# The second scan direction's steps put out eight steps behind the first one's

## The chip, the cores and the metric

The kernel runs on one core of one Trainium2 chip. The metric is the device time of one launch in microseconds (us), the median of the runs. All engines of the core are used: TensorE (PE) multiplies, VectorE (DVE) and ScalarE (ACT) take the products out of the eight PSUM banks, and SyncE (SP) issues the weight transfers. GpSimd does nothing here.

## What is computed

The reference is two transformer blocks of two layers each, over 256 tokens and, in the second block, 256 more of context. The change touches one stage of the second block's first layer, a linear recurrence with a matrix state that is scanned forwards and backwards over the 512 tokens, 8 heads of width 64:

```python
def wkv7_scan(S0, inputs, reverse):
    def step(S, inp):
        r, w, k, v, kk, a = inp
        S = (S * w[:, :, None, :]
             - jnp.einsum('bhvk,bhk->bhv', S, kk)[..., None] * (kk * a)[:, :, None, :]
             + v[..., None] * k[:, :, None, :])
        return S, jnp.einsum('bhvk,bhk->bhv', S, r)
    ...
S_cf, y_cf = wkv7_scan(S0, dir_inputs(f_ctx, 0), reverse=False)
S_cb, y_cb = wkv7_scan(S0, dir_inputs(f_ctx, 1), reverse=True)
_, y_lf = wkv7_scan(S_cf, dir_inputs(f_lat, 0), reverse=False)
_, y_lb = wkv7_scan(S_cb, dir_inputs(f_lat, 1), reverse=True)
o_lat = rwkv7_readout(y_lf + y_lb, f_lat, r_k, gn_w, gn_b)
```

The two directions share nothing until their outputs are added.

## The kernel before

The program is a list of stages (`schedule`), and each engine runs its own part of each stage, in the order in which it is written out; at a stage's end all engines meet at a barrier. Nothing reorders work: what one engine has put in a row, it does in that row, and a wait holds everything behind it on that engine.

The recurrence stage is `wkv`. It cuts the 512 tokens into 4 pairs of chunks of 64 tokens. In each direction, every pair is first **prepared** and then **advanced** through.

Preparing a pair takes 17 steps. `tokens` (L1104) transposes two operands, taken out by ACT. Six `products` steps follow (L1117), called p00, p01, p10, p11, p20, p21 here (the kind, then the half). ACT copies a part of p00 and p01 and DVE masks the rest; after p01 DVE also makes four wide masks (L2078 to L2081), and only then is level 0 ready. Then a 64x64 triangular inverse is built in five levels. Each level is an `inner` step (PE at L1092, then ACT's copy at L1563) and an `outer` step (PE at L1092, then DVE's two subtractions at L2106 and L2108). The outer needs the inner's copy, and the next inner needs DVE's subtractions. DVE also makes a mask in each inner (L2097).

Advancing takes 8 steps: `x` (L1154, L1161), `u` (L1165), `state` (L1170, L1171) and `y` (L1176, L1181, L1183), for each of the two chunks. u needs ACT's copy of x, state needs ACT's copy of u and is taken out by DVE (L2117, L2119), x of the next chunk needs that state.

`one_way` writes the steps of one direction: it prepares pair 0, and then puts the 17 preparing steps of the next pair between the 8 advancing steps of this one. That makes 100 steps a direction, 25 for each of the first three pairs' advance, 17 before them and 8 behind them. With x0, u0, s0, y0 for the first chunk's steps, x1, u1, s1, y1 for the second's, and in1, out1 and so on for the levels, a period of 25 reads

```
x0 tokens p00 | u0 p01 p10 | s0 p11 p20 | y0 p21 in1 | x1 out1 in2 | u1 out2 in3 | s1 out3 in4 | y1 out4 in5 out5
```

`wkv_order` merges the two directions (L686 to L688), and PE, ACT and DVE all three walk through its list. Before the change every step of direction 0 is followed at once by the same step of direction 1. Each step takes the next of the eight PSUM banks in turn, and PE waits before a step until that bank has been read by ACT or DVE. The step that is meant is written with its direction below, as in in2(0).

In the rows of the trace, a buffer's name tells the direction: sq, rs, tmp, rstd, rec_kt, rec_rt, rec_lw and ms belong to direction 0; mix_small, rec_lora, rec_spare, rec_kk, rec_r and rec_k to direction 1.

Of the kernel before, what the change touches and what calls it, by code (L numbers as in the profile page):

```python
# [404 lines left out]
def build(nc, ins, out):  # L405
    order = weight_order()
    with ExitStack() as ctx:
# [253 lines left out]
        def wkv_order():  # L661


            def prepare(i):
                yield ("tokens", i)
                for k in range(3):
                    for half in range(2):
                        yield ("products", i, k, half)
                for lvl in range(1, LEVELS):
                    for what in ("inner", "outer"):  # L670
                        yield (what, i, lvl)

            def advance(i):
                for n in range(2):
                    for what in ("x", "u", "state", "y"):
                        yield (what, i, n)

            def one_way():
                yield from prepare(0)
                for i in range(4):  # L680
                    ahead = list(prepare(i + 1)) if i < 3 else []
                    for k, this in enumerate(advance(i)):
                        yield this
                        yield from ahead[len(ahead) * k // 8:len(ahead) * (k + 1) // 8]

            for step in one_way():  # L686
                for d in range(2):
                    yield (d, *step)  # L688


        def by_head(h):
# [40 lines left out]
        def _(pe):  # L732
# [351 lines left out]
            def wkv():  # L1084

                def small(bank, lhs, rhs, part=lambda t: t):
# [6 lines left out]
                    return mm  # L1093

                for d, what, i, *more in wkv_order():
                    pair, halves, way, vt = wkv_pairs(d)[i], wkv_halves(d), scan[d], ph3["vt"]
                    lw, bt, kt, rt = way["lw"], way["bt"], way["kt"], way["rt"]
# [112 lines left out]
        def _(act):  # L1210
# [329 lines left out]

            def wkv():
                for d, what, i, *more in wkv_order():
                    halves, way = wkv_halves(d), scan[d]
                    if what == "tokens":
# [68 lines left out]
        def _(dve):  # L1613
# [439 lines left out]
            def wkv():  # L2053
# [6 lines left out]

                begun = set()
                for d, what, i, *more in wkv_order():
                    way, st = scan[d], scan[d]["state"]
                    nt, m, mt, b = way["nt"], way["m"], way["mt"][i % 2], way["b"]
# [213 lines left out]
```

## Time and profile before

| | us |
|---|---|
| median of 3 runs | 3096.91 |
| lowest and highest run | 3082.44, 3098.36 |
| the profiled execution | 3097.93 |
| its span on the core | 3096.1 |
| PE busy | 2667.8 (86%) |
| DVE busy | 1522.3 (49%) |
| ACT busy | 897.5 (29%) |
| the recurrence stage on PE, from its first to its last weight load | 1460.1 to 1724.5 |

Times below are counted from the span's start. PEld is the row of TensorE's weight loads: every matmul has one ahead of it, and the loads are issued in program order, so their starts show when PE came to a step. An f32 matmul of 64 rows is two records in the trace. A bracket at a row's end says how long the engine had stood idle and for whom. The granted clock is TensorE's, as a share of 2.4 GHz: 1.00 is 2.4 GHz and 0.50 is 1.2 GHz, and means between them mix the two.

### The profile page before, as it was taken

Reading aid. Unit: us, or ns where it says so; the run is one execution under the profiler, and the core shown is the slowest. Engines: PE = TensorE matmul, PEld = TensorE weight load, DVE = VectorE, ACT = ScalarE, POOL = GpSimd, SP = SyncE. Lnnn points to the kernel's source line nnn. Section 1 sums busy time; section 2 is a strip of 40 time slices with the busy share of each in tenths; the row PEclk is TensorE's granted clock in tenths of the full one; section 3 lists DMA queues with packets and bytes.
Section 4 is the critical chain, followed back from the end, with each engine's and each line's share of the span. In section 5 each row is a group of like instructions: output and inputs, shape, how many; then the busy total and the mean of one; then the engine's idle time right before and its main releaser. Section 6 shows DMA issues by size and latency. Waiting matters only on the chain.

```text
span 3096.1 us, 41660 instructions
## 1 busy us (share of the span) xinstructions
PE 2667.8 (86%) x17514; PEld 2078.2 (67%) x17514; DVE 1522.3 (49%) x2510; ACT 897.5 (29%) x1541; POOL 0.2 (0%) x4
## 2 busy tenths in 40 slices
PE   6947788688999967973999789999899998979898
PEld 5715666366888744742999448887688875736897
DVE  4674554715553255778444455542333323285544
ACT  1132011314222234334222132222422223244543
POOL 0000000000000000000000000000000000000000
PEclk9967989799999987976899899999999999989999
DMA  6700554033433220320000124332222222101443
GB/s 252 270 2 29 202 205 189 14 109 109 150 136 123 95 97 1 123 95 1 3 4 4 55 109 143 131 135 102 75 95 96 94 96 83 68 1 55 150 165 135
DMA packets 43418, 309.72 MB, mean 100 GB/s; under 512 B 4704, under 2 KB 6112, under 8 KB 6368
## 3 DMA queue, kind: packets, MB, share of 16 engines
q1 hardware_dynamic: 41328, 300.24, 26.7%
q10 hardware_dynamic: 1904, 6.80, 0.6%
q8 instruction: 140, 2.29, 0.3%
q14 instruction: 46, 0.38, 0.0%
HBM read 305.98 MB, written 1.05 MB: 99 GB/s over the span
## 4 chain that ended last, share of the span: by engine, by line
PEld 29%; PE 23%; DVE 12%; issue 10%; ACT 6%; DMA 0%; PEldq 0%; DVEq 0%; ACTq 0%
PEld bank L1031 10%; PEld bank L1038 10%; PEld bank L1034 9%; PE bank L1092 3%; PE bank L862 3%; PE bank L938 1%; ACT hn L1370 1%; PE bank L957 1%; PE bank L1031 1%; DVE ms L1644 1%; PE bank L1034 1%; PE bank L1038 1%; ACT w_hi L1346 1%; PE bank L988 1%; PE bank L835 1%
## 5 line engine op out<-in xcount | busy, mean ns | idle before, releaser
L1727 DVE TENSOR_TENSOR w_lo<-ring,w_hi 128x1024 fp32r<-128x1024 f32 (+1 forms) x264 | 315.0, 1193 | 639.1 <-ACT w_hi L1346 639.1
L1031 PE MATMUL bank<-ffn_x_hi,w_hi 128*128 128x512 f32 (+1 forms) x1344 | 498.2, 371 | 4.8 <-DVE w_lo L1727 3.8
L1034 PE MATMUL bank<-ffn_x_lo,w_hi 128*128 128x512 f32 (+1 forms) x1344 | 493.9, 367 | 0.0
L1038 PE MATMUL bank<-ffn_x_hi,w_lo 128*128 128x512 f32 (+1 forms) x1344 | 493.8, 367 | 0.0
L1644 DVE SCALAR_TENSOR_TENSOR ms<-ring,c_silu 128x1024 f32<-128x1024 f32 x288 | 352.1, 1223 | 98.0 <-DMA ring<-in_stream 93.0
L1346 ACT ACTIVATE w_hi<-ring 128x1024 fp32r<-128x1024 f32 (+1 forms) x264 | 271.6, 1029 | 336.6 <-PE bank L1034 323.3
L1031 PEld LDWEIGHTS bank<-ffn_x_hi,w_hi 128*128 128x128 f32 x1344 | 253.1, 188 | 58.0 <-DVE w_lo L1727 10.9
L1034 PEld LDWEIGHTS bank<-ffn_x_lo,w_hi 128*128 128x128 f32 x1344 | 253.1, 188 | 46.3
L1038 PEld LDWEIGHTS bank<-ffn_x_hi,w_lo 128*128 128x128 f32 x1344 | 253.1, 188 | 46.3
L1031 PE MATMUL bank<-ffn_h_hi,w_hi 128*128 128x512 f32 (+1 forms) x704 | 263.2, 374 | 1.5 <-DVE w_lo L1727 1.0
L1038 PE MATMUL bank<-ffn_h_hi,w_lo 128*128 128x512 f32 (+1 forms) x704 | 258.6, 367 | 0.0
L1034 PE MATMUL bank<-ffn_h_lo,w_hi 128*128 128x512 f32 (+1 forms) x704 | 258.6, 367 | 0.0
L862 PE MATMUL bank<-hn,ring 128*128 128x256 f32 (+1 forms) x784 | 184.4, 395 | 20.2 <-DMA ring<-in_stream 8.9
L862 PEld LDWEIGHTS bank<-hn,ring 128*128 128x128 f32 x784 | 151.0, 195 | 53.1 <-issue 16.8
L1031 PEld LDWEIGHTS bank<-ffn_h_hi,w_hi 128*128 128x128 f32 x704 | 132.5, 188 | 29.6 <-DVE w_lo L1727 3.1
L1034 PEld LDWEIGHTS bank<-ffn_h_lo,w_hi 128*128 128x128 f32 x704 | 132.6, 188 | 25.4 <-issue 1.4
L1038 PEld LDWEIGHTS bank<-ffn_h_hi,w_lo 128*128 128x128 f32 x704 | 132.6, 188 | 24.2
L1481 ACT ACTIVATE ffn_h_hi<-rs 128x512 fp32r<-128x512 f32 (+1 forms) x88 | 50.9, 579 | 326.0 <-DVE rs L1967 326.0
L1475 ACT ACTIVATE sq<-bank 128x512 f32<-128x512 f32 (+1 forms) x88 | 47.9, 545 | 246.1 <-PE bank L1038 246.1
L1967 DVE TENSOR_TENSOR rs<-bank,sq 128x512 f32<-128x512 f32 (+1 forms) x88 | 54.9, 624 | 85.1 <-PE bank L1038 55.3
L1816 DVE SCALAR_TENSOR_TENSOR x<-bank,modv,x 128x256 f32<-128x256 f32 x80 | 35.8, 480 | 117.0 <-PE bank L862 70.8
L835 PE MATMUL bank<-mix_in_x_hi,mix_in_w_hi 128*128 128x512 f32 x152 | 63.6, 418 | 25.4 <-DVE mix_in_x_lo L1745 18.6
(413 smaller groups left out, 3743.6 us busy)
## 6 DMA issues: line engine op xcount, KB each, us to landing
ring<-in_stream SPq DMA_DIRECT2D x283, 1024.0 KB, 4.8
x<-in_x SPq DMA_DIRECT2D x1, 2048.0 KB, 8.6
one_const<-in_one ACTq DMA_DIRECT2D x1, 1665.0 KB, 11.1
mix_const<-in_two ACTq DMA_DIRECT2D x1, 1440.0 KB, 6.1
win_const<-in_win ACTq DMA_DIRECT2D x1, 1089.0 KB, 5.0
c_silu<-in_c SPq DMA_DIRECT2D x1, 1024.0 KB, 10.6
out<-hn ACTq DMA_DIRECT2D x1, 1024.0 KB, 4.8
mix_small<-in_small_two ACTq DMA_DIRECT2D x1, 768.0 KB, 7.6
```

Source lines behind the costliest of these rows:

```text
L835: mm = pe.matmul(bank[:, :], high[:, kc, :], hi, start=kc == 0, stop=False)
L862: mm = pe.matmul(bank[:, 0:tok], w[:, kc * COLS + m * P:kc * COLS + (m + 1) * P], a[:, kc, 0:tok], start=kc == 0, stop=kc == KC - 1)
L1031: mm = pe.matmul(bank[:, 0:tok], high[:, kc, :], hi, start=k == 0, stop=False)
L1034: mm = pe.matmul(bank[:, 0:tok], high[:, kc, :], lo, start=False, stop=False)
L1038: mm = pe.matmul(bank[:, 0:tok], low[:, kc, :], hi, start=False, stop=last)
L1092: mm = pe.matmul(part(bank[r, col]), lhs[r, col], part(rhs[r, col]), start=True, stop=True)
L1346: nc.scalar.activation(place(n)[0][:, 0:h.nk, :], raw_half(h), ACT.Copy).then_inc(sem("w_hi_ready"), 1)
L1475: nc.scalar.activation(ffn_gate[:, h.c % 2, 0:tok], bank[:, 0:tok], ACT.Silu).then_inc(sem("gate_ready"), 1)
L1481: nc.scalar.activation(ph5["h_hi"][:, h.c, 0:tok], ffn_hidden[:, h.c % 2, 0:tok], ACT.Copy).then_inc(sem("hidden_hi"), 1)
L1644: link(V.scalar_tensor_tensor(ms2[:].rearrange("p a b -> p (a b)"), w, 1.0, c_silu[:, part % 2, :], ALU.mult, ALU.mult, accum_out=dst))
L1727: V.tensor_tensor(low[:, 0:h.nk, :], raw_half(h), high[:, 0:h.nk, :].bitcast(F32), ALU.subtract).then_inc(sem("w_split"), 1)
L1967: V.tensor_tensor(ffn_hidden[:, h.c % 2, 0:tok], bank[:, 0:tok], ffn_gate[:, h.c % 2, 0:tok], ALU.mult).then_inc(sem("product_ready"), 1)
```

## The change

```diff
-            for step in one_way():
-                for d in range(2):
-                    yield (d, *step)
+            steps = list(one_way())
+            lag = len(list(prepare(0))) // 2
+            for k in range(len(steps) + lag):
+                if k < len(steps):
+                    yield (0, *steps[k])
+                if k >= lag:
+                    yield (1, *steps[k - lag])
```

`prepare(0)` has 17 steps, so the lag is 8. The first 8 steps of direction 0 and the last 8 of direction 1 have no partner; in between, step k of direction 0 is followed by step k - 8 of direction 1. The steps, their instructions and the order within each direction stay as they are. All lines below L692 move down by four.

On PE at the start of the stage, from the last of the products on, there stands before

```order
L1117 MATMUL bank<-rec_r,rec_bt 64x64 x8
L1092 MATMUL bank<-sq,rs 64x64 x16
L1092 MATMUL bank<-mix_small 64x64 x16
L1092 MATMUL bank<-rs,tmp 64x16x2 x16
L1092 MATMUL bank<-tmp,rs 64x16x2 x16
L1092 MATMUL bank<-rec_lora,rec_spare 64x16x2 x16
L1092 MATMUL bank<-rec_spare,rec_lora 64x16x2 x16
L1092 MATMUL bank<-sq,rs 64x64 x16
```

and now

```order
L1121 MATMUL bank<-rec_rt,rec_bt 64x64 x16
L1096 MATMUL bank<-sq,rs 64x64 x16
L1096 MATMUL bank<-rs,tmp 64x16x2 x16
L1096 MATMUL bank<-tmp,rs 64x16x2 x16
L1108 MATMUL bank<-base,rec_k 128x128 x4
L1108 MATMUL bank<-base,rec_bt 128x128 x4
L1096 MATMUL bank<-sq,rs 64x64 x16
L1121 MATMUL bank<-rec_kk,rec_bt 64x64 x8
L1121 MATMUL bank<-rec_bt,rec_kk 64x64 x8
```

Between in1(0) and out1(0) the other direction's in1 is gone and nothing stands in its place; between out1(0) and in2(0) there are the transposes of direction 1 and no longer its out1.

On PE in the period of a later pair, around x1(0) and in2(0), there stands before

```order
L1154 MATMUL bank<-rec_vt,mix_o 64x64 x8
L1161 MATMUL bank<-mix_const,rec_kt 64x64 x8
L1154 MATMUL bank<-rec_vt,rec_spare 64x64 x8
L1161 MATMUL bank<-ring,rec_kk 64x64 x8
L1092 MATMUL bank<-rs,rstd 64x16x2 x16
L1092 MATMUL bank<-rstd,rs 64x16x2 x16
L1092 MATMUL bank<-rec_lora,rec_spare 64x16x2 x16
L1092 MATMUL bank<-rec_spare,rec_lora 64x16x2 x16
L1092 MATMUL bank<-sq,rs 64x64 x16
```

and now

```order
L1158 MATMUL bank<-rec_vt,mix_o 64x64 x8
L1165 MATMUL bank<-mix_const,rec_kt 64x64 x8
L1121 MATMUL bank<-rec_kk,rec_bt 64x64 x8
L1121 MATMUL bank<-rec_bt,rec_kk 64x64 x8
L1096 MATMUL bank<-rs,rstd 64x16x2 x16
L1096 MATMUL bank<-rstd,rs 64x16x2 x16
L1121 MATMUL bank<-rec_kk,rec_k 64x64 x8
L1121 MATMUL bank<-rec_r,rec_k 64x64 x8
L1096 MATMUL bank<-sq,rs 64x64 x16
```

p01(1) has come to stand ahead of out1(0), and p10(1), not out1(1), is what lies between out1(0) and in2(0).

On DVE at the same place, the subtractions of out1(0) (tile rstd) are reached before through

```order
L2097 TENSOR_TENSOR rs<-sq,mix_const 128x512
L2097 TENSOR_TENSOR mix_small<-mix_const 128x512
L2106 TENSOR_TENSOR sq<-sq,bank 128x128x2
L2108 TENSOR_TENSOR rstd<-rstd,bank 128x128x2
L2106 TENSOR_TENSOR mix_small<-mix_small,bank 128x128x2
L2108 TENSOR_TENSOR rec_spare<-rec_spare,bank 128x128x2
```

and now through

```order
L2101 TENSOR_TENSOR rs<-sq,mix_const 128x512
L2079 TENSOR_TENSOR mix_small<-bank,mix_const 128x256
L2082 TENSOR_TENSOR rec_spare<-mix_const 128x512
L2083 SCALAR_TENSOR_TENSOR mix_small<-mix_small,mix_const 128x512
L2084 TENSOR_TENSOR mix_small<-mix_const 128x512
L2085 SCALAR_TENSOR_TENSOR rec_spare<-rec_spare,mix_const 128x512
L2110 TENSOR_TENSOR sq<-sq,bank 128x128x2
L2112 TENSOR_TENSOR rstd<-rstd,bank 128x128x2
```

The five operations of p01(1), its part and the four wide masks, now stand directly ahead of the subtractions of out1(0).

## Rows read from the trace of the kernel before

**Rows 1.** The profile's 40 slices of 77.4 us: PE busy, granted clock, in tenths.

```profile
PE   6947788688999967973999789999899998979898
...
PEclk9967989799999987976899899999999999989999
```

**Rows 2.** Windows over the stage, by pair: us, busy by engine, clock, DMA.

```profile
1460.10:1512.10 52.00, 49.12 (x1297) 47.98 (x1297) 24.46 (x52) 10.48 (x19) 0.00 (x0) 0.83 0.01 3
1512.10:1576.70 64.60, 62.33 (x1745) 60.41 (x1744) 29.09 (x62) 14.62 (x26) 0.00 (x0) 0.95 0.01 4
...
1706.50:1724.60 18.10, 17.71 (x445) 16.75 (x443) 4.67 (x11) 4.14 (x7) 0.00 (x0) 1.00 0.01 3
```

**Rows 3.** Who weight loads waited for in the stage: us in total, times, longest.

```profile
PEld bank L1176 <- DVEq L2089: 4.3, 3, 1.7
PEld bank L1092 <- issue: 3.8, 15, 0.3
...
PEld bank L1092 <- DVEq L2089: 2.5, 1, 2.5
```

**Rows 4.** Timeline of weight loads at pair 1: start us, us, what.

```profile
1541.85 1.02 PEld L1092 LDWEIGHTS bank<-rec_lora,rec_spare 64*64 64x64 f32 x32
...
1543.72 1.02 PEld L1092 LDWEIGHTS bank<-sq,rs 64*64 64x64 f32 x32
1544.99 1.04 PEld L1092 LDWEIGHTS bank<-mix_small 64*64 64x64 f32 x32 [0.25 <-issue]
1545.95 0.89 PEld L1165 LDWEIGHTS bank<-ms,tmp 64*64 64x64 f32 x14
```

**Rows 5.** Timeline of DVE behind out1(1) at 1543.7 us.

```profile
1543.96 0.42 DVE L2106 TENSOR_TENSOR mix_small<-mix_small,bank 128x256 f32<-128x256 f32 x1 [1.11 <-PE bank L1092]
1544.30 0.42 DVE L2108 TENSOR_TENSOR rec_spare<-rec_spare,bank 128x256 f32<-128x256 f32 x1
```

**Rows 6.** Timeline of ACT behind in2(1) at 1545.95 us.

```profile
1546.20 0.60 ACT L1563 ACTIVATE rec_lora<-bank 128x512 f32<-128x512 f32 x1 [0.69 <-PE bank L1092]
```

**Rows 7.** Timeline of weight loads at x0(0), x0(1) and p00.

```profile
1507.84 1.01 PEld L1154 LDWEIGHTS bank<-rec_vt,mix_o 64*64 64x64 f32 x16
...
1509.80 0.19 PEld L1154 LDWEIGHTS bank<-rec_vt,rec_spare 64*64 64x64 f32 x2
...
1513.97 0.54 PEld L1117 LDWEIGHTS bank<-rec_kt,rec_bt 64*64 64x64 f32 x16 [0.17 <-issue]
...
1514.90 0.55 PEld L1117 LDWEIGHTS bank<-rec_kk,rec_bt 64*64 64x64 f32 x16
```

**Rows 8.** Timeline of DVE at p01(0)'s and p01(1)'s parts and behind.

```profile
1519.26 0.42 DVE L2075 TENSOR_TENSOR sq<-bank,mix_const 128x256 f32<-128x256 f32 x1 [2.06 <-ACT sq L1559]
...
1522.68 0.42 DVE L2075 TENSOR_TENSOR mix_small<-bank,mix_const 128x256 f32<-128x256 f32 x1 [0.22 <-DVE rstd L2081]
...
1525.19 0.68 DVE L2081 SCALAR_TENSOR_TENSOR rec_spare<-rec_spare,mix_const 128x512 f32<-128x512 f32 x1
1526.02 0.76 DVE L2086 TENSOR_TENSOR mix_o<-bank,mix_const 128x256 f32<-128x256 f32 x2
```

**Rows 9.** Timeline of weight loads at p20(1), y0(0) and y0(1).

```profile
1525.02 0.55 PEld L1117 LDWEIGHTS bank<-rec_r,rec_bt 64*64 64x64 f32 x16
1526.89 0.55 PEld L1176 LDWEIGHTS bank<-rec_rt,mix_const 64*64 64x64 f32 x16 [1.31 <-DVEq L2089]
...
1528.56 0.86 PEld L1176 LDWEIGHTS bank<-rec_r,ring 64*64 64x64 f32 x15
```

**Rows 10.** Windows between changes of the granted clock, columns as in Rows 2.

```profile
1474.10:1487.70 13.60, 12.92 (x242) 12.93 (x244) 8.00 (x19) 1.79 (x3) 0.00 (x0) 0.50 0.01 2
...
1528.70:1535.50 6.80, 6.72 (x132) 6.54 (x126) 5.03 (x13) 0.34 (x1) 0.00 (x0) 0.50 0.01 2
...
1593.50:1600.40 6.90, 6.83 (x132) 6.64 (x130) 5.13 (x13) 0.60 (x1) 0.00 (x0) 0.51 0.01 2
...
1658.40:1665.20 6.80, 6.73 (x131) 6.54 (x126) 5.00 (x13) 0.39 (x1) 0.00 (x0) 0.50 0.01 2
```

## The prediction

> **What bounds the kernel now.** I read the page's 40 slices first. The stage lies in slices 19 to 22 (1460 to 1725 us), with PE busy in 7 to 9 tenths there and the clock between 0.8 and 0.9 [rows 1]. So PE is the bound of the stage, and time can only come or go by PE's waits and by its clock. The windows by pair say the same: of the 64.6 us of a period PE is busy for 62.3, while DVE has 29.1 and ACT 14.6, and the clock's mean is 0.95 [rows 2]; the period repeats three times, within 0.4 us. Then I read what PE waits for. In the list of waits of the weight loads there are three of up to 1.7 us at y0 for a bank that DVE still holds, fifteen of some 0.25 us before an inner, and one of 2.5 us before the first inner [rows 3]. Last I read the clock: it stood at 1.2 GHz for 13.6 us and three times for 6.8 us [rows 10], each time just after one of the four long waits. All else in the program (1460 us before the stage and 1371 behind it) is closed off by barriers and runs the same instructions, so I count it at nothing.
>
> **What a step costs and how long its results take.** At 2.4 GHz an outer issues in 1.87 us (1541.85 to 1543.72), an inner in 0.95 (1544.99 to 1545.95) and x in 2.0, p00 in 0.93 (1513.97 to 1514.90) and y in 1.7 [rows 4, 7, 9]; p20 and p21 have half of p00's matmuls, about 0.4, and u and state I take at 0.85 (u has half of an inner's matmuls at twice the spacing). The chains: out1(1) is issued by 1543.72, DVE starts on it 0.24 later, its two subtractions take 0.76, and in2(1) starts at 1544.99 [rows 4, 5]. **An outer thus needs 1.27 us behind its end until the same direction's next inner may start.** In2(1) is issued by 1545.95 and ACT's copy runs from 1546.20 to 1546.80 [rows 4, 6], so **an inner needs about 1.0 us until its outer**. And p01 holds DVE for 3.34 us in a row (1522.68 to 1526.02) [rows 8].
>
> **The wait at each place is the chain less what the other direction puts in between.** In lockstep an outer(0) has outer(1) behind it (1.87, more than 1.27), so direction 0 never waits; outer(1) has only inner(0) behind it (0.93), so direction 1 waits 0.35, sixteen times: 5.6 us. The three waits at y0 are 1.45, 1.45 and 1.8, read as the start of y0(0) less the issue of p20(1) (1525.02 + 0.42 to 1526.89 for the first) [rows 9]: 4.7. The start has 2.6, and a few tenths at the changes to transposes and in the tail add about 3. Together **16 us of waits** before.
>
> With the lag, walking through the order and subtracting:
>
> - Start. in1(0) now waits only for one direction's masks, 1.7 us; out1(0) has nothing ahead of it, 1.0; in2(0) has the transposes, 0.4; then in3 0.4, in4 1.7 (DVE is busy with p01(1)'s masks), out4 0.6, in5 0.9 and four of 0.15. Sum 7.1.
> - Direction 1's first levels against p00, u0, p01 and s0 of direction 0: 0.4, 0.4, 1.7 (p01(0)'s masks again) and four of 0.15. Sum 3.1.
> - Direction 0 in each of three periods: in2(0) has only p10(1) in between and DVE comes to out1(0) only behind p01(1). With p01(1) issued at T, DVE starts its part at T + 0.9 (ACT's copy comes first: 0.25 until it starts [rows 6], some 0.4 at half the width, and the hand-over), is free at T + 4.2, level 1 is ready near T + 5.2; PE has out1(0) and p10(1), 2.8, so it waits 2.5. in3(0) has p20(1) in between: 0.9; in4(0) and in5(0) have an inner(1) each: 0.35 each; out5(0) has u1(1): 0.2. Sum 4.3, three times 12.8.
> - Direction 1 in two periods: in2 and in3 have an outer and an x, no wait; in4 has u0(0), 0.4; in5 has s0(0), and DVE is again behind p01(0)'s masks, 1.4; out5 0.15. Sum 2.0, twice 4.0. The last period, beside direction 0's last steps, 0.7.
> - Tail. The last 8 steps of direction 1 run alone. The chains x to u and u to state stand bare, about 1.0 each, two of each, and a few tenths at x1. Sum 4.3. Before, the two directions covered each other there: 18.1 us with PE busy for 17.7 [rows 2].
> - What goes: the three waits at y0, since DVE gets p01 of the two directions apart, and the sixteen of 0.35.
>
> **32 us of waits after, 16 before: +16 us.** No instruction is added, and neither SP's queue nor a transfer is touched: the two transfers that wait for the end of the scan still wait for it.
>
> **The clock.** A stretch at 1.2 GHz issues matmuls at 53 ns a record where 30 is the rule (12.9 busy us for 244 records, against 32 in 0.95) [rows 4, 10], so it loses about 0.45 of its length: before, 34.1 us at 1.2 GHz cost 15. After the change I count eight waits of 1.4 us or more (two at the start, one in direction 1's first levels, three of 2.5, two of 1.4), before only four. No row shows what a wait of 2.5 us in mid-stage does, but the 1.45 us one at 1525.4 was enough for 6.8 us at 1.2 GHz and the 2.6 us one for 13.6. The bounds for the added part: nothing (the new waits drop the clock no more often than the old ones did), and 8 x 13.6 less 34.1 = 75 us more at 1.2 GHz, 34 us lost. Four more stretches of 6.8 would lose 12; since a slower PE also covers part of the chains I take **+11 us**.
>
> Sum: 16 + 11 = +27 us on the profiled 3097.93, and from the median of 3096.91 **3124 us**.
>
> The Trainium skill, "TensorE: Matmul & The Clock Gate", section "Why this matters for your kernels", says that throughput drops come from idle gaps of PE that are longer than any in this stage. The trace does not agree: the clock fell after 1.45 us. By that rule no wait here would cost clock, and the sum would keep its first term alone.
>
> **The rivals.**
>
> *No change (3098 us).* The lag trades the places of the dips: the long waits before were each followed by a slow stretch, and if the new ones fall so that the clock never drops, the 15 us of clock come back and pay for the 16 us of waits: +1. For it: PE is busy all around the 2.5 us wait. Against it: the wait itself is longer than those that dropped the clock before. The same result stands if DVE's masks are hidden (the 2.5 us shrink to the bare 0.35) and two thirds of the dips remain.
>
> *Faster (3078 us).* DVE's load is spread: in lockstep both directions' masks meet (1519.3 to 1526.0, with a pause of 0.2) [rows 8] and PE waits for it at y0. If that is the only wait that matters, and the short chains hide behind work that PE has queued, the waits fall from 16 to 12 and all 15 us of clock come back, -19. It decides this way if no wait of the new order exceeds about 1 us. Against it: PE works in order, and 0.9 us of p10(1) cannot cover 1.27 us even with DVE free.
>
> *Much slower (3145 us).* The start and each period stay at 1.2 GHz for long, because the waits come every few us and the levels between them did not bring the clock back for 13.6 us once before [rows 10]. The upper bound above: +16 + 34 = +50, 3147.
>
> That the change doesn't do what it says is no rival here: the order of all three engines shows the lag.
>
> **How the numbers follow.** Forecast (slower, waits and some more clock, 3108 to 3136): 0.52. Much slower: 0.20. No change: 0.20. Faster: 0.08. The range leaves out the faster case and the far end of the slowest: 3098 to 3148. A measurement of this kernel can tell about 0.5% (15 us) from no change; the forecast's low end and the no-change case lie within that, so faster 0.06, same 0.24, slower 0.70.
>
> **What would show it.** In the profile after: the stage from its first weight load to its last takes about 291 us, not 264; in1(0) starts some 7 us sooner; three weight loads of an inner (sq) wait for DVE for about 2.5 us, none at L1180 for more than a few tenths; direction 1 runs alone for about 15 us at the end. If instead the list of waits shows no wait above 1 us, the DVE step is wrong; if the waits are as said and the total is not, the clock term is.

## The result: 57 us slower, beyond the range

| | before | after |
|---|---|---|
| median | 3097.16 us (4 runs) | 3153.93 us (4 runs) |
| lowest and highest | 3082.44, 3098.36 | 3147.71, 3157.22 |
| the recurrence stage, first to last weight load | 264.4 us | 312.0 us |
| of it at 1.2 GHz | 37.8 us | 117.3 us |

The ratio is 1.0192, 95% interval 1.0157 to 1.0227. The forecast was +27 us with a range up to 3148, so the direction was right and the size was not. The clock's part is in every run, not only in the profiled one: the granted clock over the whole program was 0.905 to 0.908 in the four runs of the change, and 0.916 to 0.927 in 69 of the 71 runs of before that stand beside the experiments (the other two were over 5% slower, and no ratio counts them).

The head of the page of after:

```profile
span 3155.4 us, 41660 instructions
PE 2712.4 (86%) x17514; PEld 2118.3 (67%) x17514; DVE 1523.1 (48%) x2510; ACT 898.0 (28%) x1541; POOL 0.2 (0%) x4
PE   6947788689999968973999689999899998979898
PEclk9967999799999987976788799999999999979999
```

The instructions are as many as before, 41660. PE is busy for 44.6 us longer, and where [rows 1] had 8, 9, 9, 8 in the clock's slices 19 to 22 there is now 7, 8, 8, 7. The profiled span grew by 59.3 us. The stage has 47.6 of them. The stage began 8.0 us later (1468.1 against 1460.1) and what lies behind it took 3.7 us longer (1375.3 against 1371.6), with the same instructions in both places. In the profiles of all fourteen kernels of this study the stage began between 1451.4 and 1468.1, whatever the kernel, so I count neither to the change. That leaves 9 us of the 57 in the medians unplaced. A profile shows one execution: in the other twelve kernels, what the stage gained or lost in the profile differs by -4 to +10 us from what the medians did, so differences of a few us between stages are not to be leaned on.

The windows of the stage (stretch, length, busy us and instructions of PE, PEld, DVE, ACT and POOL, clock, DMA share, GB/s): start up to the first x0(0), three periods from x0(0) to x0(0), the rest while both directions run, and direction 1 alone.

```profile
1468.10:1509.20 41.10, 36.81 (x879) 35.38 (x879) 18.94 (x40) 7.51 (x14) 0.00 (x0) 0.75 0.01 3
1509.20:1586.40 77.20, 72.04 (x1767) 69.86 (x1764) 29.18 (x62) 15.23 (x27) 0.00 (x0) 0.82 0.01 3
1586.40:1662.20 75.80, 71.05 (x1754) 68.85 (x1751) 29.14 (x62) 14.64 (x26) 0.00 (x0) 0.82 0.01 3
1662.20:1738.30 76.10, 71.42 (x1752) 69.21 (x1748) 29.09 (x62) 14.64 (x26) 0.00 (x0) 0.82 0.01 3
1738.30:1759.70 21.40, 20.95 (x599) 20.10 (x595) 7.46 (x17) 4.16 (x7) 0.00 (x0) 1.00 0.02 4
1759.70:1780.10 20.40, 17.43 (x257) 16.08 (x257) 2.54 (x6) 2.37 (x4) 0.00 (x0) 0.64 0.01 2
```

Against [rows 2]: the start is 6.6 us shorter (47.7 before), the three periods together are 34.7 us longer (229.0 against 194.3), and from x0(0) of the last pair to the end it is 19.5 us longer (41.8 against 22.3). A period has the same instructions on DVE and ACT, busy for the same 29 and 15 us. PE has the same instructions too, but takes 72 us for what took it 62, at a clock of 0.82 where it was 0.95. The whole stage, before and after:

```profile
1460.10:1724.50 264.40, 253.96 (x6975) 246.08 (x6976) 116.41 (x249) 58.38 (x104) 0.00 (x0) 0.93 0.01 3
1468.10:1780.10 312.00, 289.70 (x6974) 279.48 (x6976) 116.35 (x249) 58.54 (x104) 0.00 (x0) 0.81 0.01 3
```

Of the 47.6 us, PE is busy in 35.7 and idle in 11.9.

The stretches at 1.2 GHz inside the stage, each as a window:

```profile
1478.60:1485.40 6.80, 6.80 (x98) 6.40 (x100) 2.04 (x5) 1.19 (x2) 0.00 (x0) 0.50 0.01 2
1495.60:1505.80 10.20, 9.63 (x172) 9.39 (x174) 3.14 (x8) 0.94 (x2) 0.00 (x0) 0.50 0.01 3
1546.80:1574.10 27.30, 26.52 (x466) 26.20 (x467) 8.76 (x19) 2.98 (x5) 0.00 (x0) 0.50 0.01 2
1621.90:1649.20 27.30, 25.36 (x455) 25.05 (x456) 9.04 (x22) 2.48 (x5) 0.00 (x0) 0.50 0.01 2
1680.00:1683.40 3.40, 3.40 (x74) 3.40 (x71) 0.58 (x2) 0.60 (x1) 0.00 (x0) 0.51 0.00 0
1700.40:1724.30 23.90, 23.30 (x426) 22.95 (x425) 7.20 (x18) 1.84 (x4) 0.00 (x0) 0.50 0.01 3
1765.30:1780.10 14.80, 13.25 (x189) 12.31 (x185) 2.12 (x5) 1.18 (x2) 0.00 (x0) 0.50 0.01 2
```

They sum to 113.7 us, where [rows 10] has 34.1. In each, PE is busy for 90% of the time or more: this is hardly waiting, but working at half speed. With the forecast's own 0.45 us lost per us, the 79.6 us more are **36 us**, which is what PE's busy time grew by. The stage's other 12 us are waits. (The totals in the table also have the end of a slow stretch that began in the stage ahead and reached 3.6 us into this one, 3.7 us before.)

The waits of the weight loads in the stage (what waits, for whom; us in total, times, longest):

```profile
PEld bank L1096 <- issue: 20.7, 24, 2.5
...
PEld bank L1169 <- ACT rec_lora L1574: 1.7, 2, 0.9
PEld bank L1174 <- ACT rec_lora L1582: 1.7, 2, 0.9
```

The waits for a bank at y0, 4.3 us in [rows 3], are gone. The inner and outer line has 20.7 us in place of 6.3, the longest 2.5. One of its three long waits in the timelines of PEld and of DVE (start, duration, what, and in brackets the idle time before it):

```profile
1543.90 0.56 PEld L1121 LDWEIGHTS bank<-rec_r,rec_k 64*64 64x64 f32 x16
1546.94 1.57 PEld L1096 LDWEIGHTS bank<-sq,rs 64*64 64x64 f32 x27 [2.48 <-issue]
```

```profile
1542.58 0.42 DVE L2079 TENSOR_TENSOR mix_small<-bank,mix_const 128x256 f32<-128x256 f32 x1 [3.43 <-ACT mix_const L1563]
1543.16 0.69 DVE L2082 TENSOR_TENSOR rec_spare<-mix_const 128x512 f32<-128x512 f32 x1
...
1545.09 0.69 DVE L2085 SCALAR_TENSOR_TENSOR rec_spare<-rec_spare,mix_const 128x512 f32<-128x512 f32 x1
1545.92 0.42 DVE L2110 TENSOR_TENSOR sq<-sq,bank 128x256 f32<-128x256 f32 x1
1546.26 0.41 DVE L2112 TENSOR_TENSOR rstd<-rstd,bank 128x256 f32<-128x256 f32 x1
```

PE has issued p10(1) and stands before in2(0), whose operand sq comes from DVE's subtractions behind out1(0). DVE reaches these at 1545.92, since it is in the part and the four wide masks of p01(1) from 1542.58 on. From the last load of p10(1) to the first of in2(0), the three periods show 2.62, 2.61 and 2.62 us. The forecast had 2.5, by this mechanism. Waits are given like this in what follows, from the start of one load to the start of the next; the idle time in the brackets and lists is about 0.13 us less, since the first load's own time is off it.

### The profile page after: what moved, and what is told of

Read it like the earlier page. It is cut to its first block, busy times and chain, and to the rows that moved or that the text cites. A ratio compares the mean times of both kernels' runs of the same rounds, so it can differ in the third digit from the quotient of the medians.

```text
span 3155.4 us, 41660 instructions
## 1 busy us (share of the span) xinstructions
PE 2712.4 (86%) x17514; PEld 2118.3 (67%) x17514; DVE 1523.1 (48%) x2510; ACT 898.0 (28%) x1541; POOL 0.2 (0%) x4
## 4 chain that ended last, share of the span: by engine, by line
PEld 28%; PE 24%; DVE 11%; issue 10%; ACT 6%; DMA 1%; PEldq 0%; DVEq 0%; ACTq 0%
PEld bank L1035 9%; PEld bank L1042 9%; PEld bank L1038 9%; PE bank L1096 4%; PE bank L866 3%; PE bank L942 1%; PE bank L1035 1%; PE bank L961 1%; ACT hn L1374 1%; PE bank L1038 1%; PE bank L1042 1%; DVE ms L1648 1%; PE bank L1121 1%; ACT w_hi L1350 1%; PE bank L992 1%
## 5 line engine op out<-in xcount | busy, mean ns | idle before, releaser
L1479 ACT ACTIVATE sq<-bank 128x512 f32<-128x512 f32 (+1 forms) x88 | 48.0, 545 | 247.4 <-PE bank L1042 247.4
L1820 DVE SCALAR_TENSOR_TENSOR x<-bank,modv,x 128x256 f32<-128x256 f32 x80 | 35.7, 480 | 117.6 <-PE bank L866 71.3
```

The source lines that it names most:

```text
L1479: nc.scalar.activation(ffn_gate[:, h.c % 2, 0:tok], bank[:, 0:tok], ACT.Silu).then_inc(sem("gate_ready"), 1)
```

## The experiments

The question is where the 30 us beyond the forecast come from, and whether the waits are their cause. The **clock theory** says: the waits cost what was forecast (+16), the rest is the clock, which the waits make fall. The **mask theory** says that the DVE block ahead of in2(0) is the root of the three long slow stretches. Times at 1.2 GHz below leave out the tail of the stretch that reaches in from the stage ahead, which was between 3.5 and 20.5 us long in these profiles and began before any instruction of this stage. Ratios are against the kernel before, with 95% intervals; the medians of before were 3096.4, 3096.6 and 3099.9 us in the three groups of runs (lag8_fill, lag8_late, lock_fill, lag6; then lock_hold, lock_fill2, lag2_start, lag6_fill; then lag8_after, lag8_fill_tail, lag7, lag2_fill).

### Does the clock cost it: PE kept busy in the waits

```diff
+def keep_busy(bank, n):
+    for k in range(n):
+        h, c = k // 2 % 8, k % 2
+        r = slice(c * C, (c + 1) * C)
+        pe.matmul(bank[r, by_head(h)], ident[r, 0:C], ones[r, 0:C], start=True, stop=True)
 ...
     bank, full = take_bank()
+    keep_busy(bank, {(0, 1, 2): 40, (0, 2, 2): 40, (0, 3, 2): 40,
+                     (1, 0, 5): 20, (1, 1, 5): 20, (1, 2, 5): 20}.get((d, i, lvl), 0))
```

This is `inner`, ahead of its wait for the level; the real matmuls overwrite the bank.

> The changed kernel with small matmuls that nobody reads put ahead of PE's wait in two inner steps: 40 (about 2.3 us at 2.4 GHz) before in2(0) of pairs 1 to 3, 20 (1.2 us) before in5(1) of pairs 0 to 2. Theory 'the clock': the waits for DVE stay as long as they are, but PE is not idle in them, so the three stretches of 24 to 27 us at 1.2 GHz do not come; 78 us x 0.45 = 35 us less than the changed kernel, about 3119 us, ratio to the kernel before 1.007. Rival 'the chain': PE is held by DVE and the clock only follows; then filling changes nothing, 3154 us, ratio 1.018.

Measured: 1.0083 [1.0061, 1.0106], median 3121.0 us. The loads of the first of the three places:

```profile
1541.37 2.47 PEld L1094 LDWEIGHTS bank<-base 64*64 64x64 f32 x80
1543.92 0.89 PEld L1102 LDWEIGHTS bank<-sq,rs 64*64 64x64 f32 x28
```

In2(0) comes as late behind p10(1) as it did, but 28 of its loads now take 0.89 us (32 ns each) where 27 took 1.57 above (58 ns), and the stretches of 27, 27 and 24 us are gone. What stays at 1.2 GHz is 3.4 and 10.2 at the start, 3.4 and the tail. The stage takes

```profile
1465.30:1746.50 281.20, 269.61 (x7333) 259.59 (x7335) 116.34 (x249) 58.55 (x104) 0.00 (x0) 0.92 0.01 3
```

281.2 us, 30.8 less than with the change, although 180 matmuls were added and no wait was taken away. That is the clock's part, with the waits left as they were: 33 us in the medians, less what the fillers themselves cost.

The tail, where x, u and state of direction 1 stand bare, was then filled too:

```diff
+    if d == 1 and i == 3 and what in ("u", "state"):
+        early = take_bank()
+        keep_busy(early[0], 14)
```

Here, in the products and in lag6_fill's tail, `keep_busy` stands for the same loop written out in place; the step then uses the bank that was taken early.

> lag8_fill with 14 more fillers in each of u and state of direction 1's last pair, where that direction runs alone. Theory 'bare tail at 1.2 GHz': the slow stretch that began 18 us before the end goes, 18 x 0.45 = 8 us less than lag8_fill: 3113 us, ratio 1.0055, stage 273 us. Rival 'the tail is held by the bare chains alone': ratio 1.008 as lag8_fill.

Measured: 1.0052 [1.0035, 1.0068], 3113.9 us, as expected for the median (the stage takes 278 us and not 273), with no slow stretch in the tail. The stage has only 10.2 us at 1.2 GHz:

```profile
1465.00:1743.10 278.10, 269.23 (x7446) 259.98 (x7448) 116.31 (x249) 58.56 (x104) 0.00 (x0) 0.95 0.01 4
```

Taking 0.45 of all time at 1.2 GHz off both (37.8 us before, 30.6 here, the reach from the stage ahead included), before has 247.4 us and this kernel 264.3. So **+17 us is what the lag costs at 2.4 GHz** (the fillers that don't fit into their wait are in it). The forecast's term of waits was +16. As both numbers come from one profile each, and the wait before in1(0) was 0.64 us in this one and 2.07 in that of the changed kernel, the agreement to 1 us is partly luck.

### Does DVE's block cause it: the wide masks behind the subtractions

```diff
-    if half: wide_masks(d, i)
+    if half and i == 0 and d == 0: wide_masks(d, i)
+    elif half: pending.append((d, i))
 ...
 # outer, behind its two subtractions
+    while pending: wide_masks(*pending.pop(0))
```

> The changed kernel with DVE's four wide masks of p01 put behind the next outer's subtractions on DVE (not for pair 0 of direction 0). Theory 'the masks': the waits of 2.6 us at in2(0) fall to the bare 0.4, those of 1.2 to 1.6 at in4(0) and in5(1) too, and the slow stretches behind them go: 3 x 2.2 + 4 x 0.9 + 35 = 45 us less, about 3109 us, ratio 1.004. Rival 'DVE is short of time': the masks come late for their own inner and PE waits there instead; then at most 10 us less, 3144 us.

Measured: 1.0061 [1.0042, 1.0079], 3115.7 us: the mask theory holds, 38 us of its 45 came. The periods take 68.4, 62.6 and 63.8 us instead of some 76, and the three long stretches are gone: between the start, with 17.1 us at 1.2 GHz, and the tail there are 3.4 us twice.

```profile
PEld bank L1096 <- issue: 13.4, 28, 1.5
```

The rest shows where it went: the masks now stand ahead of the next outer's subtractions, so in3(0) waits 1.45 us, three times, where it waited 0.93.

### Does the size of the lag decide: lags of six and seven

```diff
-            lag = len(list(prepare(0))) // 2
+            lag = 6
```

> The changed kernel with a lag of 6 steps instead of 8. Walking through its order as in the prediction gives 19 us of waits (before: 16), none over 1.5 us, since p01(1) no longer stands ahead of out1(0). Theory 'where DVE's masks fall decides': slow stretches as few as before, 3097 us within 8, ratio 1.000. Rival 'any lag costs, for its bare ends and for the mixing of unlike steps': 6/8 of the 57 us, 3140 us, ratio 1.014.

Measured: 1.0011 [0.9994, 1.0028], 3098.5 us: no difference from before. The windows of one period and of the stage, and the waits:

```profile
1500.00:1561.30 61.30, 59.34 (x1743) 57.26 (x1740) 29.12 (x63) 15.24 (x27) 0.00 (x0) 1.00 0.01 4
```

```profile
1457.60:1719.80 262.20, 251.71 (x6973) 241.93 (x6975) 115.85 (x249) 58.55 (x104) 0.00 (x0) 0.94 0.01 4
```

```profile
PEld bank L1096 <- issue: 9.7, 25, 1.4
```

With six steps of lag p01(1) stands ahead of in1(0), with p10(1), x1(0) and s0(1) between it and out1(0). No wait is longer than 1.51 us, and all three periods run at a clock of 1.00: 60.9, 61.3 and 61.4 us, against 64.7 in lockstep. That is 10 us gained in the periods; the tail gives them back, 36.2 us from x0(0) of the last pair against 22.3, of which direction 1 runs 16.0 alone.

And with seven:

```diff
-            lag = len(list(prepare(0))) // 2
+            lag = 7
```

> The changed kernel with a lag of 7. The same walk through its order gives waits of 2.3 to 2.5 us behind DVE's masks four times and 26 us of waits in all (lag 6: 19, lag 8: 32). Theory 'waits of over 2 us bring slow stretches in the lagged order': 10 us for waits and 10 to 20 for the clock, 3120 us, ratio 1.008, between lag6 (1.001) and lag 8 (1.019). Rival 'lag 8 is a special meeting of steps': as lag6, ratio 1.001.

Measured: 1.0181 [1.0149, 1.0212], 3154.5 us, not 3120. The waits were as reckoned: 2.34 at the start and 2.40, 2.61, 2.61 in the periods, before the inners behind an outer whose subtractions stand behind wide masks. The slow stretches were 17.1, 23.9, 13.7, 68.3 us and the tail. Two of them:

```profile
1597.50:1611.20 13.70, 13.57 (x193) 12.75 (x190) 2.94 (x8) 2.39 (x4) 0.00 (x0) 0.50 0.01 2
1665.80:1734.10 68.30, 67.57 (x1116) 66.03 (x1117) 18.91 (x42) 8.51 (x15) 0.00 (x0) 0.50 0.01 2
```

Two waits of 2.61 us, one followed by 13.7 us at 1.2 GHz and the other by 68.3, with PE busy for 99% of both. The two waits:

```profile
1596.91 1.35 PEld L1096 LDWEIGHTS bank<-mix_small 64*64 64x64 f32 x32 [2.48 <-issue]
1666.12 1.81 PEld L1096 LDWEIGHTS bank<-mix_small 64*64 64x64 f32 x32 [2.48 <-issue]
```

They are in5(1) of pairs 1 and 2, and the same 40 steps follow both; the second stretch ends before these are over. So **neither the wait nor the steps behind it fix the length**: both were the same here, in one execution. What differed is not shown. I had again priced a wait by stretches of other places, and was again too low by about 35 us.

### What sets the length of a slow stretch: the wait or what follows it

First the wait alone, in the lockstep order. Four DVE operations that change nothing (a maximum of a mask with itself) stand ahead of the subtractions behind out1(0) of pairs 1 to 3, as the wide masks do in the changed kernel:

```diff
     if d == 0 and i and lvl == 1:
+        for _ in range(4): link(V.scalar_tensor_tensor(m, m, 1.0, m, ALU.mult, ALU.max))
```

> The kernel before, in lockstep, with four wide operations of 0.7 us (m = max(m, m), which change nothing) put on DVE ahead of the subtractions of out1(0) in pairs 1 to 3, as long as the four masks that the lag puts there. PE should then wait about 2.3 us at in2(0), three times. Theory 'such a wait brings a long stretch at 1.2 GHz wherever it stands': beside the 6.8 us ones behind y0 there come three more of 14 us or more, as behind the 2.6 us wait at the stage's start; 3 x 2.3 + 3 x 14 x 0.45 = 26 us, about 3122 us, ratio 1.008; with stretches of 27 us as in the changed kernel 3140 us, 1.014. Rival 'it takes the lagged order as well': only the waits count, 7 us, 3103 us, ratio 1.002.

Measured: 1.0057 [1.0036, 1.0077], 3114.2 us. The hold, the wait in the stage's list, and the slow stretches behind it:

```profile
1540.09 2.87 DVE L2106 SCALAR_TENSOR_TENSOR sq<-sq 128x512 f32<-128x512 f32 x4 [5.07 <-PE bank L1092]
```

```profile
PEld bank L1092 <- issue: 9.7, 15, 2.2
```

```profile
1543.80:1547.20 3.40, 3.15 (x60) 3.18 (x61) 1.45 (x3) 0.60 (x1) 0.00 (x0) 0.50 0.02 5
1612.00:1615.40 3.40, 3.35 (x63) 3.38 (x64) 1.44 (x3) 0.60 (x1) 0.00 (x0) 0.50 0.00 0
1680.30:1683.70 3.40, 3.17 (x60) 3.20 (x62) 1.44 (x3) 0.60 (x1) 0.00 (x0) 0.50 0.02 5
```

Waits of 2.36, 2.35 and 2.36 us before the same in2(0), and the clock is back after 3.4 us, not after 27. In lockstep in2(0) is followed by in2(1) and by both directions' u. The statement that such a wait brings a long stretch wherever it stands falls with this. The rival, that only the waits count (3103 us), doesn't hold either: the three short stretches came too. The stage takes 274.5 us, 10.1 more than before, and the medians 17.6 more; the difference is within what one profile can be off. The wait here is 0.26 us shorter than in the changed kernel, so the next kernel keeps the wait and changes only what follows it:

```diff
     bank, full = take_bank()
     pe.wait_ge(level_ready, ...)
+    keep_busy(bank, 56 if (d, lvl) == (0, 2) and i else 0)
```

> The changed kernel with 56 filler matmuls (64x64, back to back) put behind PE's wait in in2(0) of pairs 1 to 3, not into it: PE stands idle for 2.6 us as before, and then has 6 us of dense work at 1.2 GHz that nobody needs. Theory 'what follows the wait holds the clock down': with dense work the clock is back after 7 to 10 us and not after 27; 3 x 18 x 0.45 = 24 us back, 3 x 5 us of fillers added, 3145 us, ratio 1.016, and the stretches seen in the trace are 7 to 10 us. Rival 'the length of the idle time sets the length of the slow stretch': stretches of 27 us again, +15 to +18 us for the fillers, 3170 us, ratio 1.024.

Measured: 1.0142 [1.0115, 1.0169], 3141.6 us. The waits are 2.61, 2.62 and 2.61 us, as with the change. The slow stretches behind them:

```profile
1543.20:1546.60 3.40, 3.40 (x71) 3.40 (x68) 0.13 (x1) 0.00 (x0) 0.00 (x0) 0.50 0.02 5
1611.50:1618.30 6.80, 5.69 (x107) 5.72 (x109) 1.50 (x4) 0.00 (x0) 0.00 (x0) 0.50 0.00 0
1683.20:1686.60 3.40, 3.05 (x58) 3.08 (x60) 0.81 (x3) 0.00 (x0) 0.00 (x0) 0.50 0.02 5
```

13.6 us together instead of 78.5, although each place issues 56 matmuls more, behind the wait and in nobody's shadow. **Behind the same wait PE stays at 1.2 GHz for 3.4 to 6.8 us with independent matmuls next, and for 24 to 27 us without them.** The fillers are matmuls of their own, back to back with no result to wait for. In the changed kernel in2(0) is followed by s0(1), u1(0), p11(1) and a lone outer, and in3(0) then waits again (0.93 us) for what out2(0) leaves. That what follows can shorten the stretch is shown; that it alone sets the length is not, by the two stretches of lag7.

### The lockstep order with its own waits filled

If waits cost clock, before must gain from fillers too. 40 stand before in1(0) of pair 0 and 24 ahead of p20(1) of pairs 1 to 3, which is before the waits at y0:

```diff
     bank, full = take_bank()   # products
+    if i and d == 1 and k == 2 and half == 0: keep_busy(bank, 24)
```

> The kernel before, both directions in lockstep, with the same fillers: 40 before in1(0) of pair 0 and 24 small matmuls ahead of p20(1) of pairs 1 to 3, where PE would soon wait at y0 for DVE. Theory 'the clock': its four stretches at 1.2 GHz (34 us) go, 15 us less: 3082 us, ratio 0.995. Rival: the waits alone count, 3097 us, ratio 1.000.

Measured: 0.9985 [0.9971, 1.0], 3090.5 us: the stage 255.3 us, the waits at y0 and their slow stretches gone, but in1(0) still waits 2.59 us and the clock falls for 6.8 us. That wait is for a bank, and the fillers stood behind it. So they went one step ahead, into p21(1) of pair 0:

```diff
+    if d == 1 and k == 2 and half == (0 if i else 1): keep_busy(bank, 24 if i else 40)
```

> Lockstep with fillers as in lock_fill, but those of the start stand in p21(1) of pair 0, so ahead of the wait for the bank at in1(0), and not behind it. The wait of 2.6 us should all but go and no stretch at 1.2 GHz be left in the stage but the one it starts in: 34 us x 0.45 = 15 us less than before, stage about 250 us, ratio 0.995; lock_fill had 0.9985. Rival: PE's clock is not what the start costs, ratio as in lock_fill.

Measured: 0.9976 [0.9962, 0.999], 3089.5 us. In1(0) no longer waits, but in2(0) does, for 1.81 us:

```profile
1473.47 1.04 PEld L1092 LDWEIGHTS bank<-sq,rs 64*64 64x64 f32 x32 [1.68 <-issue]
```

The clock held for 5.6 us behind it, and then was at 1.2 GHz for 3.4. The stage:

```profile
1451.40:1705.10 253.70, 247.42 (x7197) 239.79 (x7199) 115.95 (x249) 58.38 (x104) 0.00 (x0) 0.99 0.02 4
```

10.7 us shorter than [rows 2] and nearly all at 2.4 GHz. In the medians 7.1 us are left of the 15 that I had expected. The profiled execution was the fastest of the twelve.

### Small lags, and a lag of six with its waits filled

The lag is 2, and the wide masks of p01(1) of pair 0 go behind the subtractions of out1(0):

```diff
-            lag = len(list(prepare(0))) // 2
+            lag = 2
 ...
-    if half: wide_masks(d, i)
+    if half and not (i == 0 and d == 1): wide_masks(d, i)
+    elif half: pending.append((d, i))
```

> The changed kernel with a lag of 2, and with the four masks of p01(1) of pair 0 put behind out1(0)'s subtractions on DVE, where the walk shows a wait of 4.3 us at in2(0) otherwise. Walk: no wait above 1.5 us in the periods (y0 no longer meets both directions' masks), a bare tail of 2 steps. Theory 'it is the place of DVE's masks': periods of 61.4 us as in lag6 instead of 64.7, start and tail near the kernel before; 3 x 3.3 = 10 us less than before, 3087 us, ratio 0.997. Rival 'the start pays it back': ratio 1.000, as lag6.

Measured: 1.0001 [0.9985, 1.0016], 3097.9 us. Periods 60.5, 60.5 and 60.9, the start 48.1, the tail 25.9. A wait of 1.86 us at the start is followed by 13.7 us at 1.2 GHz. The three periods together are 12 us shorter than in lockstep and the tail 3.6 longer; the stage was 8 us shorter in the profile, but the medians show nothing of it.

The lag of six, with fillers (as above) ahead of its waits:

```diff
+    keep_busy(bank, {(0, 0, 1): 12, (0, 0, 2): 8, (0, 0, 3): 24, (0, 0, 4): 12,
+                     (0, 1, 3): 12, (0, 2, 3): 12, (0, 3, 3): 12}.get((d, i, lvl), 0))
 ...
+    if d == 1 and i == 3 and what in ("u", "state"):
+        early = take_bank()
+        keep_busy(early[0], 14)
```

> The changed kernel with a lag of 6 and fillers of 0.4 to 1.4 us at its waits: in1 to in4(0) of pair 0, in3(0) of the other pairs, and u and state of direction 1's bare tail. Theory 'the clock': its two stretches at 1.2 GHz (10.2 us at the start, 7 of 13.7 in the tail) go, 8 us less than lag6, stage 254 us, 3089 us, ratio 0.997. Rival: the bare chains at both ends hold it at lag6's 262 us, ratio 1.001.

Measured: 0.9996 [0.9983, 1.001], 3096.0 us: no wait above 1 us, no new slow stretch, the stage 258.8 us, and no difference from before. PE is busy for 253.3 of these us, the fillers included, and nearly all at 2.4 GHz, so there is little left to fill.

The lag of two as in lag2_start, its masks moved too, with fillers ahead of its waits:

```diff
 # products
+    if i and d == 1 and k == 2 and half == 0: keep_busy(bank, 14)
 ...
 # inner
+    keep_busy(bank, {(1, 0, 1): 28}.get((d, i, lvl), 0))
```

> lag2_start with fillers: 28 before in1(1) of pair 0 (its wait of 1.9 us) and 14 in p20(1) of pairs 1 to 3. The slow stretch of 13.7 us at the start goes, 6 us less, stage 250 us; ratio 0.998 beside lag2_start's 1.000. If a lag is worth anything over lockstep once the clock is held, this is below lock_fill2 (0.9976); if not, equal or above.

Measured: 0.997 [0.9951, 0.9988], 3088.3 us. The stage:

```profile
1459.70:1715.70 256.00, 250.21 (x7113) 241.39 (x7115) 116.08 (x249) 58.55 (x104) 0.00 (x0) 0.95 0.01 4
```

20.5 of its 256.0 us are the stretch from the stage ahead, which was 3.7 us in before. This kernel and `lock_fill2` are the fastest of the study (the second is the lockstep order with 112 fillers); their intervals overlap, and between them nothing is decided.

## Why the prediction was wrong in size, step by step

| step | forecast | measured |
|---|---|---|
| in2(0) in a period | 2.5 us | 2.62, 2.61, 2.62 |
| in3(0) | 0.9 | 0.93 |
| in5(1) of pair 0 | 1.7 | 1.28 |
| in5(1) of pairs 1 and 2 | 1.4 | 1.30, 1.24 |
| waits at y0 | gone | gone |
| in1(0) after the stage's start | 7 us sooner | 6.2 (8.45 against 14.65) |
| x to u and u to state, tail | 1.0 each | 0.95 to 1.09 |
| direction 1 alone | 15 us | 20.4, of it 14.8 at 1.2 GHz |
| waits at 2.4 GHz, net | +16 | +17 (lag8_fill_tail less before, in the profiles) |
| clock | +11 | +36 (79.6 us x 0.45; PE busy 35.7 longer) |
| stage | 291 us | 312 |

**What bounds the kernel** held: PE, by its waits and its clock. **The waits** held, each in its place and cause. Subtracting what the other direction puts in between from the chain's length gave in2(0), in3(0) and in5(1) of pairs 1 and 2 to within 0.2 us, and in5(1) of pair 0 and in1(0) at the start to within 0.5 (2.07 us measured before in1(0), 1.7 forecast). Two sums of the walk are slightly off: the terms of the start add up to 7.3 and not 7.1, and three times 4.3 is 12.9; the total stays at 32. The 47.6 us of the stage are 36 of clock and 12 of waits; that the waits' part is under 17 goes the way that the forecast gave, since a slower PE covers more of each chain: in1(0) waited 2.07 us where PE came to it at 2.4 GHz (the changed kernel), and 0.64 where it came at 1.2 (lag8_fill, lag8_fill_tail). These 5 us were not taken apart.

**The step that failed is the clock term**, "+11 us", with its bound of 75 us more at 1.2 GHz: 79.6 came. It took the number of long waits (eight) times the length of a slow stretch in lockstep (6.8, at most 13.6 us). The number was nearly right: five waits reached 1.4 us, the three at in5(1) had 1.24 to 1.30, and there were six stretches, behind six of these eight waits, and the tail. The length was wrong, and so was its bound, since both were read from a single order of steps. `lag8_fill` shows that this is the term: with the waits as they were and PE kept busy in them, 33 us went. `lock_hold` and `lag8_after` show that the length depends on what stands behind the wait, which the change rearranges, and lag7 that this is not all of it. Of the 30 us beyond the forecast the clock term has 25, the waits have -4, and the other 9 are those that lie outside the stage. I had noticed that no row showed what a 2.5 us wait does in mid-stage; the right consequence would have been a wider upper end.

**The rivals.** *Faster* fell: the load on DVE is spread and y0 no longer waits, but the waits in the levels are longer than those. *No change* fell for this lag. Its picture is what a lag of six does, where p01 meets no critical subtraction: the lags of six and eight differ by 55 us, and one of seven is as slow as eight. *Much slower* is what came, with its reason (the start and the periods stay at 1.2 GHz for long), at 3154 and not 3145. It had 0.20; the 13.6 us stretch of [rows 10], which followed a wait while the other stretches had half of that, was the sign that one length doesn't fit all.

The rule of the Trainium skill that the prediction weighed ("TensorE: Matmul & The Clock Gate", section "Why this matters for your kernels") would have left the clock term at nothing. The runs bear out the trace against it: no wait in the stage was longer than 2.62 us, and filling waits of 1.3 to 2.6 us gave back 33 us.

## What stays open

How the clock comes back is not settled. Shown is that it came back within 3.4 to 6.8 us where matmuls with no wait among them followed, and that it stayed down for 27.3 and 68.3 us with PE busy for 97% and 99%. The same wait with the same steps behind it gave 13.7 and 68.3 us in lag7. The steps at the start are the same in the changed kernel, lag8_fill, lag8_after and lag8_fill_tail, and yet the stage's first 41 us had 20.6, 24.4, 30.3 and 30.5 us at 1.2 GHz, the stretch from the stage ahead included. Each kernel's stretches were seen in one execution. What in the lagged order holds it down (the lone outers, the short waits between them, the spacing of u) was not taken apart. Nor is it shown why the fillers' gain in the lockstep order is 7 us in the medians and 10.7 in the stage of the profile; the stage ahead varies by more than that from run to run.

## What to carry to other kernels

When two dependent chains are interleaved on one in-order engine, first look on the *other* engines for long blocks of one chain (here 3.3 us of DVE masks) that land ahead of the other chain's critical operation: one step of lag more or less decides. A lag that looks symmetric also buys bare ends, where each chain runs alone. And don't price a clock drop by the wait that starts it or by a stretch seen elsewhere, be it in the same kernel: keep the upper end wide, and if the wait can't be removed, put independent matmuls into it. That took 33 us from the changed kernel and 7 from the one before.

## What the runs showed of the hardware

- The wait and the length of the stretch at 1.2 GHz behind it are not in proportion: 2.36 us gave 3.4 (lock_hold), 2.61 gave 13.7 in one place and 68.3 in another of lag7 with the same steps behind both, 1.86 gave 13.7 (lag2_start), 1.45 gave 6.8 (before) or, in lag8_late, 3.4 once and nothing once.
- A PE that is 99% busy with small f32 matmuls can stay at 1.2 GHz: 67.6 busy us of 68.3 in lag7.
- Matmuls whose results nobody needs shortened a kernel: 180 of them took the stage from 312.0 to 281.2 us, and the median from 3153.9 to 3121.0 (lag8_fill).
